# Moving solve steps, gate stores and row loads, and unscaled keys with a per-token factor on DVE in the delta rule

## The chip, the cores and the metric

The kernel runs on one core of a Trainium2 chip. The metric is the device time in microseconds of one execution, as the median of several. PE is TensorE, DVE VectorE, ACT ScalarE, POOL GpSimd, SP SyncE, which here issues all DMA.

## The reference

One layer of a streaming encoder, float32: a prompt of 4096 frames of width 1024, and 8 running streams with 16 new frames each. Two head groups of 8 heads of 64 run side by side; group A is a gated delta rule, group B softmax attention over a band of nine chunks of 64. The part that matters is group A for the prompt, in 64 chunks of 64 frames:

```python
gc = jnp.cumsum(g, axis=-1)
decay = jnp.exp(jnp.where(incl, gc[..., :, None] - gc[..., None, :], -jnp.inf))
kk = jnp.einsum('bhnid,bhnjd->bhnij', k, k)
lower = jnp.where(strict, beta[..., :, None] * kk * decay, 0.0) + jnp.eye(blen, dtype=f32)
rhs = jnp.concatenate([v * beta[..., None], k * (beta * jnp.exp(gc))[..., None]], axis=-1)
sol = lax.linalg.triangular_solve(lower, rhs, left_side=True, lower=True)
u, w = sol[..., :dv], sol[..., dv:]
qk = jnp.einsum('bhnid,bhnjd->bhnij', q, k) * decay
q_dec = q * jnp.exp(gc)[..., None]
k_tail = k * jnp.exp(gc[..., -1:] - gc)[..., None]
g_tot = jnp.exp(gc[..., -1])
def step(s, xs):                      # one chunk
    v_new = u_c - jnp.einsum('bhld,bhde->bhle', w_c, s)
    o_c = jnp.einsum('bhld,bhde->bhle', qd_c, s) + jnp.einsum('bhij,bhje->bhie', qk_c, v_new)
    s = s * gt_c[..., None, None] + jnp.einsum('bhld,bhle->bhde', kt_c, v_new)
    return s, o_c
```

q and k are L2-normed; k's norm enters as a factor per token.

## The kernel before

The kernel is a row of phases, each a block of five instruction streams that meet at semaphores, with a barrier between them. Every matmul of the projections is done as three products of float32 parts (`matmul3`, lines 88 to 90).

**Phase A** (`project_a`, to 782 us in the profile) projects q, k, v and the gates of group A, 256 tokens per block, does the convolution, and stores the activations (`qkvB`), the products k k^T and q k^T (`kq`), the sums of squares of the queries (`ssqT`), and per head and chunk the summed decays (`gcC`) and betas (`betaC`). `store_gates` writes these last two; the chunks lie in DRAM in the order of `slot(n)`: in 32 chunks first the 16 even ones, then the odd ones.

**Phase B** (`project_b`, 782 to 1730 us) projects the other columns for 33 tiles of 128 tokens in 165 units; a unit is one tile times 512 columns, 24 matmuls into one of five PSUM banks (`BANKS`). The units begin with Q of tiles 0 and 1, K of tiles 0 and 1, then Q and K of tile 2. Per tile SP loads x (`load_x`, line 1056), ACT rounds it (`split_hi`, line 1230), DVE takes the rest (`split_lo`, line 1315). PE waits for `lo_ok` ahead of a tile, and for `normed` of five units earlier ahead of a bank. Per Q or K unit ACT squares, DVE sums (line 1371), POOL takes the power (lines 1196, 1200), DVE scales (line 1376).

Between the units the other engines solve the triangular systems of the 64 chunks, in four groups of 16 chunks x 8 heads = 128 systems, one per partition (`solve_plan`, `solve(u)` of each stream). A planner lays out the steps: each engine has a list in fixed order, each step a cost, each unit a `budget(k, u)` per engine, and a step comes in the first unit in which its needs are planned. `PRE = 4` units (-4 to -1) lie ahead of unit 0. In them, before the change, SP issues `lgb` (decays and betas, line 1084), `lkk` (2 MB of k k^T into M, line 1090), `lqk` and `seg` (line 1109), DVE does `ssk` (line 1327, waits for `lkk`) and the two differences `dd` (line 1338), ACT `init` and `eg`, POOL the four powers `pow` (line 1165). In unit 0 DVE does `rows` (line 1345), which waits for the powers. The first `load_x` inside the units is that of tile 2, at the end of unit 2 in SP's order.

**The delta rule** (`delta`, 1730 to 2083 us) goes through 64 chunks, two per tile. SP loads per tile the factors (`sc`, line 1564: the keys' and the queries' factor per token, broadcast over 64 partitions), the solved matrices `UQ`, the gate rows `za` and per two tiles the raw q, k, v (`conv_T`, line 1554), six tiles ahead. Once, `ketr` and `ssqT` come into `rows` (lines 1582, 1583), are transposed by PE (line 1776) and copied by DVE (line 1840). Per tile POOL multiplies keys and queries by their factors (`scaled`, line 1619: `Kd`, `Qd`), gates and norms the output; PE transposes keys and values (`prepare`, lines 1716, 1718), ACT copies the values (`vt`, line 1659), DVE scales the transposed keys (`kt`, line 1808). The loop per chunk, each step for two halves of four heads: PE `Kd` x state into `psS` (`keys_state`, line 1735); DVE r = vt - psS (`residual`, line 1819); PE solves (`solved`, line 1754); ACT copies the new values (line 1668); PE takes their product with `kt` (`new_state`, line 1771); DVE adds the decayed state (`state`, line 1831). Queries times state (line 1746) and the outputs (line 1762) lie between them in PE's order; DVE sums the squares of a tile's output (`out_sums`, line 1837) after the state of its next even chunk.

Behind it come the delta rule of the samples, the attention and the output projections.

## Time and profile before

| | |
|---|---|
| median of 3 runs | 3701.06 us (3700.84 to 3708.35) |
| profiled execution | 3700.53 us, span 3698.8 us |
| mean granted TensorE clock | 0.961 |
| PE busy | 3406.3 us, 92% of the span |
| DVE busy | 2123.7 us, 57% |
| ACT busy | 1388.1 us, 38% |
| POOL busy | 1023.8 us, 28% |

The span runs from the first to the last instruction of the slowest core. An engine is busy while it works on data; waits are not counted. In a row of a timeline the first number is the start, the second the time to the end of the group, "x2" the number of instructions in it, and the bracket holds how long the engine had been idle and whose result came last ("issue": no releaser found). PEld is the loading of weights into TensorE. The clock is granted in parts of full speed, 1.00 being 2.4 GHz and 0.50 1.2 GHz.

### The profile page before, as it was taken

The numbers are of one execution on the slowest core, as the hardware profiler recorded it, in microseconds if no ns is written. First come the engines' busy times: TensorE is split into PE (matmuls) and PEld (weight loads), VectorE is DVE, ScalarE is ACT, GpSimd is POOL, SyncE is SP. The second block draws the span as 40 slices with busy tenths as digits, with TensorE's granted clock in tenths as the row PEclk, the third lists the DMA queues.
The fourth block names the chain that finished last, engine by engine and source line by source line (L and its number), as shares of the span: only waits on it lengthen the run. The fifth ranks groups of instructions, "written<-read, shape, count | busy, mean of one in ns | idle before, by whom it ended". The sixth has DMA issues, their size and how long they took to land. (4 is left out here: it accounts for less than half of the span.)

```text
span 3698.8 us, 68754 instructions
## 1 busy us (share of the span) xinstructions
PE 3406.3 (92%) x26606; PEld 2912.4 (79%) x26606; DVE 2123.7 (57%) x4024; ACT 1388.1 (38%) x2648; POOL 1023.8 (28%) x1313
## 2 busy tenths in 40 slices
PE   6999999959998999997888577999997999999998
PEld 6999899948887888885777455888885888888887
DVE  7777687747988968760344454666664233333332
ACT  5555555533223322211565424666663111111111
POOL 3222122238997644400687510000000000000000
PEclk9999999979999999998898788999998999999999
DMA  5343333355347453434987443222224121212120
GB/s 152 107 117 104 101 110 107 96 145 156 112 121 212 133 161 102 122 106 131 252 253 240 120 143 121 84 76 77 82 67 171 61 68 61 68 61 68 61 68 36
DMA packets 320091, 428.30 MB, mean 116 GB/s; under 512 B 189539, under 2 KB 204163, under 8 KB 315190
## 3 DMA queue, kind: packets, MB, share of 16 engines
q1 hardware_dynamic: 319806, 424.43, 38.0%
q8 instruction: 187, 3.06, 0.3%
q14 instruction: 98, 0.80, 0.1%
HBM read 267.51 MB, written 159.46 MB: 115 GB/s over the span
## 5 line engine op out<-in xcount | busy, mean ns | idle before, releaser
L88 PE MATMUL b_psP<-b_w_hi,b_xT_hi 128*128 128x512 f32 x1320 | 518.7, 393 | 45.3 <-DVE b_xT_lo L1315 28.2
L89 PE MATMUL b_psP<-b_w_lo,b_xT_hi 128*128 128x512 f32 x1320 | 516.4, 391 | 0.0
L90 PE MATMUL b_psP<-b_w_hi,b_xT_lo 128*128 128x512 f32 x1320 | 515.8, 391 | 0.0
L88 PE MATMUL a_psG<-a_xT_hi,a_w_hi 128*128 128x256 f32 (+1 forms) x1536 | 454.3, 296 | 21.0 <-DVE a_xT_lo L670 19.5
L89 PE MATMUL a_psG<-a_xT_lo,a_w_hi 128*128 128x256 f32 (+1 forms) x1536 | 442.0, 288 | 0.0
L90 PE MATMUL a_psG<-a_xT_hi,a_w_lo 128*128 128x256 f32 (+1 forms) x1536 | 441.3, 287 | 0.0
L88 PEld LDWEIGHTS b_psP<-b_w_hi,b_xT_hi 128*128 128x128 f32 x1320 | 249.3, 189 | 104.3 <-DVE b_xT_lo L1315 53.0
L88 PEld LDWEIGHTS a_psG<-a_xT_hi,a_w_hi 128*128 128x128 f32 x1536 | 296.0, 193 | 42.7 <-DVE a_xT_lo L670 23.5
L687 DVE SCALAR_TENSOR_TENSOR a_act<-a_raw,a_taps,a_act 128x256 f32<-128x256 f32 x576 | 288.9, 502 | 20.6
L90 PEld LDWEIGHTS a_psG<-a_xT_hi,a_w_lo 128*128 128x128 f32 x1536 | 296.3, 193 | 0.0
L89 PEld LDWEIGHTS a_psG<-a_xT_lo,a_w_hi 128*128 128x128 f32 x1536 | 296.2, 193 | 0.0
L90 PEld LDWEIGHTS b_psP<-b_w_hi,b_xT_lo 128*128 128x128 f32 x1320 | 249.5, 189 | 52.7
L89 PEld LDWEIGHTS b_psP<-b_w_lo,b_xT_hi 128*128 128x128 f32 x1320 | 249.5, 189 | 51.4
L3128 POOL TENSOR_SCALAR h_var<-h_ssq 128x1 f32<-128x1 f32 x33 | 6.3, 191 | 865.8 <-ACT h_squares L3160 865.8
L2637 DVE CUSTOM_DVE_ANT_0 f_neg<-f_score,f_bias 128x640 f32<-128x640 f32 (+4 forms) x256 | 192.4, 780 | 81.9 <-PE f_score L2537 52.9
L410 POOL COPY a_halo<-a_raw 128x3 f32<-128x3 f32 x192 | 74.1, 386 | 509.6 <-ACT a_raw L515 508.2
L88 PE MATMUL h_psH<-h_w_hi,h_mT_hi 128*128 128x512 f32 x528 | 210.0, 398 | 5.1 <-DVE h_w_lo L107 5.1
L2456 ACT ACTIVATE f_prob<-f_neg,f_low 128x640 f32<-128x640 f32 (+4 forms) x256 | 201.2, 788 | 17.9 <-DVE f_low L2637 17.9
L1036 DVE TENSOR_TENSOR b_tmp_v<-b_M,b_col_v 128x62 f32<-128x62 f32 (+28 forms) x464 | 205.7, 483 | 3.6
L90 PE MATMUL h_psH<-h_w_hi,h_mT_lo 128*128 128x512 f32 x528 | 207.1, 392 | 0.0
L89 PE MATMUL h_psH<-h_w_lo,h_mT_hi 128*128 128x512 f32 x528 | 207.0, 392 | 0.0
L90 PE MATMUL h_psG<-h_w_hi,h_hT_lo 128*128 128x512 f32 x528 | 205.5, 389 | 0.0
(365 smaller groups left out, 7373.8 us busy)
## 6 DMA issues: line engine op xcount, KB each, us to landing
rows_b<-b_rows SPq DMA_DIRECT2D x165, 256.0 KB, 2.2
b_x_full<-xT SPq DMA_DIRECT2D x78, 512.0 KB, 4.2
qkvB<-a_act SPq DMA_DIRECT2D x16, 1536.0 KB, 5.4
d_conv_T<-qkvB SPq DMA_DIRECT2D x16, 1536.0 KB, 11.9
xT<-a_x_full SPq DMA_DIRECT2D x33, 512.0 KB, 3.6
h_mixed<-mixed SPq DMA_DIRECT2D x33, 512.0 KB, 4.1
out<-h_y SPq DMA_DIRECT2D x33, 512.0 KB, 3.0
a_x<-in_x_prompt SPq DMA_DIRECT2D x32, 512.0 KB, 4.1
```

Source lines behind the costliest of these rows:

```text
L88: nc.tensor.matmul(out, x_hi, w_hi, start=first, stop=False)
L89: nc.tensor.matmul(out, x_hi, w_lo, start=False, stop=False)
L90: return nc.tensor.matmul(out, x_lo, w_hi, start=False, stop=last)
L410: pool.tensor_copy(halo[:, g, :], x[:, N:]).then_inc(halo_ok, 1)
L687: v.scalar_tensor_tensor(out, x[:, j:j + N], taps[:, j, g:g + 1], out, ALU.mult, ALU.add).then_inc(conv, 1)
L1036: eng.tensor_tensor(t, U[:, c0:c1, j:j + 1].to_broadcast([P, c1 - c0, L]), factor.unsqueeze(1).to_broadcast([P, c1 - c0, L]), ALU.mult).th ...
L2456: e.activation(prob[h % 4][:, 0:n], neg[h % 2][:, 0:n], ACT.Exp, scale=-1.0, bias=low[a.b][:, h:h + 1], accum_out=total[a.b][:, h:h + 1]). ...
L2637: v.tensor_tensor_reduce(neg[h % 2][:, 0:n], score[h % 2][:, 0:n], bias[:, h, KEYS - n:], -1.0 / ROOT, BIG, ALU.add, ALU.min, low[a.b][:, ...
L3128: g.tensor_scalar(var[:, :], ssq[:, :], 1.0 / D, EPS, ALU.mult, ALU.add).then_inc(e_var, 1)
```

## The change

1. **Gates.** `gcC` and `betaC` are stored in the natural order of the chunks, two stores each instead of four; `lgb` puts them in the order of the groups with four loads each instead of one.
2. **Solve steps.** In the units ahead of unit 0 only SP has a budget. The steps of DVE, POOL and ACT begin in unit 0. The loads of x for tiles 2 and 3 (`LEAD = 2`) go ahead of SP's first solve steps.
3. **Unscaled keys.** The tensor `kqrow` becomes `krow` and `qrow`. `sc` holds the queries' factor alone; POOL's `Kd` is gone, and `keys_state` multiplies the raw keys. `krow` comes into `rows` and is transposed with the others; DVE copies and negates it (`key_gain`), and the residual is computed as psS x (-factor of the token) + vt, one `scalar_tensor_tensor` of 64 columns per head. The wait for `g_kd` is gone; the load of raw tiles also waits for `t_sk`.
4. **Row loads.** The eight loads of `ketr` and `krow` and that of `ssqT` go ahead of the loads of tile 0.

```diff
@@ def store_gates(q):
-                    for e in range(2):
-                        for odd in range(2):
-                            at = slot(n * b + odd)
-                            sp.dma_start(there[at:at + n // 2, e * PAIRS:(e + 1) * PAIRS].rearrange("n h i -> h n i"),
-                                         x[e::2, :].rearrange("h (n o i) -> h n o i", o=2, i=C)[:, :, odd, :]).then_inc(ok, 16)
+                        sp.dma_start(there[n * b:n * (b + 1), e * PAIRS:(e + 1) * PAIRS].rearrange("n h i -> h n i"),
+                                     x[e::2, :].rearrange("h (n i) -> h n i", n=n)).then_inc(ok, 16)
@@ project_b, budget(k, u):
+        if u < 0:
+            return 100.0 if k == "sp" else 0.0
         if k == "v":
             return 4.0 if u < HEADS else 5.0
         if k == "g":
-            return 5.0 if u < 0 else 2.8 if u < HEADS else 4.8
+            return 2.8 if u < HEADS else 4.8
@@ project_b, sync, solve(u):
                     if kind == "lgb":
                         for x, src in ((gcl, d.gcC), (betal, d.betaC)):
-                            sp.dma_start(x[:, :, :], src.rearrange("(g n) h i -> (n h) g i", g=GROUPS)).then_inc(gb_in, 16)
+                            by_group = src.rearrange("(a n e) h i -> a e n h i", e=2, n=CC)
+                            for g in range(GROUPS):
+                                sp.dma_start(x[:, g, :], by_group[g // 2, g % 2]).then_inc(gb_in, 16)
@@ project_b, sync:
+            for n in range(LEAD):
+                load_x(n + 2)
             for u in range(-PRE, 0):
                 solve(u)
             for u, (n, seg) in enumerate(units):
-                if u == ends[n] and n + 2 < len(visits):
+                if u == ends[n] and LEAD <= n < len(visits) - 2:
                     load_x(n + 2)
@@ delta, sync:
             def load_raw(x):
                 if x >= 3:
                     sp.wait_ge(t_prep, 2 * (x - 2))
                     sp.wait_ge(g_qd, 2 * (x - 2))
+                    sp.wait_ge(t_sk, 2 * 2 * 2 * (x - 2))
...
+            for n in range(NCH // 16):
+                for first, src in ((0, d.ketr), (2 * H, d.krow)):
+                    there = rows[first:first + H, n // 2 * 32 * C:(n // 2 + 1) * 32 * C]
+                    sp.dma_start(there.rearrange("h (c e i) -> h c e i", e=2, i=C)[:, :, n % 2, :],
+                                 src[16 * n:16 * (n + 1)].rearrange("c h i -> h c i")).then_inc(rows_in, 16)
+            sp.dma_start(rows[H:2 * H, :], d.ssqT).then_inc(rows_in, 16)
             for t in range(BUFS):
                 if t % 2 == 0:
                     load_raw(t // 2)
                 load(t)
@@ delta, gpsimd, scaled(t):
-                for out_, x, first, done in ((Kd, 0, PAIRS, g_kd), (Qd, 1, 0, g_qd)):
+                g.tensor_tensor(Qd[t % 2]..., raw(t)[:, 0:PAIRS, :]..., sc[b][:, :, :, :], ALU.mult).then_inc(g_qd, 1)
@@ delta, tensor, keys_state(n, x):
                 pe.wait_ge(v_state, 2 * n + x + 1)
-                if x == 0 and n % 2 == 0:
-                    pe.wait_ge(g_kd, t + 1)
                 for p, e, h, at, rows_e in half_heads(x):
-                    last = nc.tensor.matmul(psS[x][c, e, p - 2 * x, :], Kd[t % 2][rows_e, p, c], old[rows_e, p, :],
+                    last = nc.tensor.matmul(psS[x][c, e, p - 2 * x, :], raw(t)[rows_e, PAIRS + p, c], old[rows_e, p, :],
@@ delta, vector, residual(n):
-                    v.tensor_tensor(r[c, at].rearrange("p (a e c) -> p e a c", a=2, e=2),
-                                    vt[t % 2][c, at].rearrange("p (a e c) -> p e a c", a=2, e=2), psS[x][c, :, :, :],
-                                    ALU.subtract).then_inc(v_r, 1)
+                    for a in range(2):
+                        for e in range(2):
+                            p = 2 * x + a
+                            cols = slice((2 * p + e) * C, (2 * p + e + 1) * C)
+                            h = e * PAIRS + p
+                            op = v.scalar_tensor_tensor(r[c, cols], psS[x][c, e, a, :], key_gain[c, t, h:h + 1], vt[t % 2][c, cols],
+                                                        ALU.mult, ALU.add)
+                    op.then_inc(v_r, 1)
@@ delta, vector, once:
-            v.tensor_copy(scal[:, :, :].rearrange("p t h -> p (t h)"), psA[:, 0:NT * 2 * H]).then_inc(v_scal, 1)
+            part = NT // 2
+            for i, src in enumerate((psA, psB)):
+                v.tensor_copy(scal[:, i * part:(i + 1) * part, :].rearrange("p t h -> p (t h)"), src[:, 0:part * 3 * H])\
+                    .then_inc(v_scal, 1)
+            v.tensor_scalar(key_gain[:, :, :], scal[:, :, 2 * H:], -1.0, None, ALU.mult).then_inc(v_key, 1)
```

## Rows read from the trace of the kernel before

**Rows 1.** Stretches: us; busy PE, PEld, DVE, ACT, POOL; PEclk, DMA share, GB/s.
```profile
782.00:1730.00 948.00, 909.53 (x3960) 746.84 (x3960) 696.52 (x1258) 265.36 (x342) 527.43 (x494) 0.98 0.46 137
1730.00:2083.00 353.00, 267.12 (x5408) 243.98 (x5408) 130.96 (x324) 183.67 (x512) 251.73 (x229) 0.87 0.75 218
```

**Rows 2.** Timeline around the start of phase B; start, us, engine, line, tiles.
```profile
761.11 0.35 SPq L299 DMA_DIRECT2D qkvB<-a_act  x1
...
793.47 1.31 SPq L1090 DMA_DIRECT2D b_M<-kq  x1
...
804.24 2.73 SPq L1056 DMA_DIRECT2D b_x_full<-xT  x2
...
807.80 0.22 DVE L1327 TENSOR_SCALAR b_kvar<-b_M 128x64 f32<-128x64 f32 x1 [8.28 <-DMA b_M<-kq]
...
808.19 13.53 POOL L1165 TENSOR_TENSOR b_rk<-b_kvar,b_neg_half 128x16 f32<-128x16 f32 x4 [26.36 <-DVE b_decays L1332]
...
821.75 0.23 DVE L1345 TENSOR_TENSOR b_krow<-b_decays,b_rk 128x64 f32<-128x64 f32 x1 [8.58 <-POOL b_rk L1165]
...
826.40 1.53 DVE L1315 TENSOR_TENSOR b_xT_lo<-b_x_full,b_xT_hi 128x1024 fp32r<-128x1024 f32 x1
...
827.99 0.80 PE L88 MATMUL b_psP<-b_w_hi,b_xT_hi 128*128 128x512 f32 x1 [15.30 <-DVE b_xT_lo L1315]
```

**Rows 3.** One stretch of 10 us, columns as in rows 1.
```profile
795.00:805.00 10.00, 10.00 (x46) 8.29 (x45) 4.52 (x8) 4.92 (x8) 0.00 (x0) 1.00 0.89 334
```

**Rows 4.** Timeline of the start of the delta rule.
```profile
1731.43 0.42 SPq L1554 DMA_DIRECT2D d_conv_T<-qkvB  x1
...
1734.99 2.72 SPq L1582 DMA_DIRECT2D d_rows<-ketr  x4
...
1737.75 2.72 SPq L1583 DMA_DIRECT2D d_rows<-ssqT  x1
...
1746.45 1.26 POOL L1619 TENSOR_TENSOR d_Kd<-d_conv_T,d_sc 128x512 f32<-128x512 f32 x1 [9.49 <-DMA d_UQ<-UQ]
...
1751.65 3.56 PE L1776 MATMUL d_psA<-d_ident,d_rows 16*128 16x16 f32 x32 [25.11 <-DMA d_rows<-ssqT]
...
1756.07 1.12 PE L1716 MATMUL d_psA<-d_ident,d_conv_T 128*128 128x128 f32 x4 [0.86 <-DVE d_scal L1840]
```

**Rows 5.** Timeline of DVE, one undisturbed tile of the delta rule.
```profile
1850.81 0.69 DVE L1837 TENSOR_REDUCE d_oss<-d_osq 128x8 f32<-128x512 f32 x1 [0.83 <-ACT d_osq L1681]
...
1859.26 0.69 DVE L1837 TENSOR_REDUCE d_oss<-d_osq 128x8 f32<-128x512 f32 x1 [0.83 <-ACT d_osq L1681]
```

**Rows 6.** Timeline of one chunk: the residual, and its second half on PE.
```profile
1863.78 0.74 DVE L1819 TENSOR_TENSOR d_r<-d_vt,d_psC 64x256 f32<-64x256 f32 x2 [0.70 <-ACT d_vt L1659]
...
1864.94 0.43 PEld L1754 LDWEIGHTS d_psC<-d_r,d_UQ 64*64 64x64 f32 x6
```

**Rows 7.** Groups by line and a timeline row: xcount, busy us, mean ns of one.
```profile
L1819 DVE TENSOR_TENSOR d_r<-d_vt,d_psC 64x256 f32<-64x256 f32 x128 | 49.0, 416 | 34.5 <-ACT d_vt L1659 20.8 <-PE d_psC L1735 12.8
...
L2968 DVE SCALAR_TENSOR_TENSOR g_both<-g_psO,g_own_inv,g_part 128x64 f32<-128x64 f32 x8 | 2.3, 284 | 0.3
...
2099.05 3.23 DVE L2201 SCALAR_TENSOR_TENSOR e_conv_T<-e_work,e_taps,e_conv_T 128x128 f32<-128x128 f32 x12
```

**Rows 8.** A disturbance on PE, and the sums of squares on DVE.
```profile
1808.16 0.69 PE L1771 MATMUL d_psC<-d_vn,d_kt 64*64 64x64 f32 x8 [3.21 <-issue]
...
1956.54 0.69 DVE L1837 TENSOR_REDUCE d_oss<-d_osq 128x8 f32<-128x512 f32 x1 [0.91 <-ACT d_osq L1681]
...
L1837 DVE TENSOR_REDUCE d_oss<-d_osq x32: 677/686/689, 1772.1 to 2075.4; 128x8 f32<-128x512 f32 x32
```

**Rows 9.** Stretches of 100 us of the delta rule, columns as in rows 1.
```profile
1757.00:1857.00 100.00, 80.73 (x1552) 73.67 (x1551) 37.18 (x92) 52.60 (x148) 66.74 (x60) 0.85 0.93 253
...
1857.00:1957.00 100.00, 82.84 (x1724) 75.14 (x1719) 41.72 (x103) 59.28 (x166) 80.84 (x73) 0.93 0.78 242
...
1957.00:2057.00 100.00, 84.42 (x1807) 77.23 (x1807) 43.44 (x108) 60.87 (x171) 83.29 (x75) 0.93 0.65 199
```

More of the change, by code:

```diff
@@ L252, in stores_of @@
         def stores_of(upto):
-            return sum(32 if b is None else 128 for b in sets[:upto])
+            return sum(32 if b is None else 64 for b in sets[:upto])
         def weights_ready(eng, upto):
@@ L1104, in solve @@
                         sp.wait_ge(v_rows, 3 * (n + 1))
-                        for x, there in ((krow, d.kqrow[:, :, 0]), (ketr, d.ketr)):
+                        for x, there in ((krow, d.krow), (ketr, d.ketr)):
                             sp.dma_start(there[chunks].rearrange("n h i -> (n h) i"), x[:, :]).then_inc(sc_out, 16)
@@ L1235, in solve @@
                     if kind == "init":
-                        e.wait_ge(gb_in, 32)
+                        e.wait_ge(gb_in, 32 * GROUPS)
                         e.activation(egl, gcl[:, :, :], ACT.Exp).then_inc(s_init, 1)
@@ L1328, in solve @@
                                         ALU.mult, ALU.add).then_inc(v_ssk, 1)
-                        v.wait_ge(gb_in, 32)
+                        v.wait_ge(gb_in, 32 * GROUPS)
                         if n:
@@ L1334, in solve @@
                     elif kind == "dd":
-                        v.wait_ge(gb_in, 32)
+                        v.wait_ge(gb_in, 32 * GROUPS)
                         if n:
@@ L1461, in delta @@
         UQ = some("UQ", [P, H, 2, C])
-        sc = some("sc", [P, 2, PAIRS, 2, C])
-        rows = ph.sb("d_rows", [2 * H, s.SEQ])
+        sc = some("sc", [P, 2, PAIRS, C])
+        rows = ph.sb("d_rows", [3 * H, s.SEQ])
         za = some("za", [P, W], ZBUFS)
-        Kd = some("Kd", [P, PAIRS, P], 2)
         Qd = some("Qd", [P, PAIRS, P], 2)
@@ L1468, in delta @@
         vt = some("vt", [P, W], 2)
-        scal = ph.sb("d_scal", [P, NT, 2 * H])
+        scal = ph.sb("d_scal", [P, NT, 3 * H])
+        key_gain = ph.sb("d_key_gain", [P, NT, H])
         S = some("S", [P, PAIRS, C], 2)
@@ L1501, in delta @@
         v_scal = ph.sem("d_v_scal")
+        v_key = ph.sem("d_v_key")
         v_kt = ph.sem("d_v_kt")
         s_vt = ph.sem("d_s_vt")
-        g_kd = ph.sem("d_g_kd")
         g_qd = ph.sem("d_g_qd")
@@ L1563, in load @@
                     half = slice(e * C, (e + 1) * C)
-                    sp.dma_start(sc[b][half, :, :, :, :],
-                                 kqrow[t // 16, :, t % 16, e * PAIRS:(e + 1) * PAIRS].partition_broadcast(C)).then_inc(ok, 16)
+                    sp.dma_start(sc[b][half, :, :, :],
+                                 qrow[t // 16, :, t % 16, e * PAIRS:(e + 1) * PAIRS].partition_broadcast(C)).then_inc(ok, 16)
                 sp.dma_start(UQ[b][:, :, :, :], d.UQ[:, :, t].rearrange("e j h x i -> (e j) h x i")).then_inc(ok, 16)
@@ L1578, in _ @@
                 load(t)
-                if t == 0:
-                    for n in range(NCH // 16):
-                        there = rows[0:H, n // 2 * 32 * C:(n // 2 + 1) * 32 * C].rearrange("h (c e i) -> h c e i", e=2, i=C)
-                        sp.dma_start(there[:, :, n % 2, :], d.ketr[16 * n:16 * (n + 1)].rearrange("c h i -> h c i")).then_inc(rows_in, 16)
-                    sp.dma_start(rows[H:2 * H, :], d.ssqT).then_inc(rows_in, 16)
             for t in range(NT):
@@ L1617, in scaled @@
                     g.wait_ge(t_qs, 2 * 2 * (t - 1))
-                for out_, x, first, done in ((Kd, 0, PAIRS, g_kd), (Qd, 1, 0, g_qd)):
-                    g.tensor_tensor(out_[t % 2][:, :, :].rearrange("p a (c i) -> p c a i", c=2),
-                                    raw(t)[:, first:first + PAIRS, :].rearrange("p a (c i) -> p c a i", c=2),
-                                    sc[b][:, :, :, x, :], ALU.mult).then_inc(done, 1)
+                g.tensor_tensor(Qd[t % 2][:, :, :].rearrange("p a (c i) -> p c a i", c=2),
+                                raw(t)[:, 0:PAIRS, :].rearrange("p a (c i) -> p c a i", c=2),
+                                sc[b][:, :, :, :], ALU.mult).then_inc(g_qd, 1)
             def gate(t):
@@ L1772, in new_state @@
                 last.then_inc(t_ds, 1)
-            pe.wait_ge(rows_in, 16 * (1 + NCH // 16))
+            pe.wait_ge(rows_in, 16 * (1 + NCH // 8))
             for t in range(NT):
-                last = nc.tensor.transpose(psA[:, t * 2 * H:(t + 1) * 2 * H], rows[:, t * P:(t + 1) * P], ident[0:2 * H, 0:2 * H])
+                to = (psA, psB)[t // (NT // 2)]
+                at = t % (NT // 2) * 3 * H
+                last = nc.tensor.transpose(to[:, at:at + 3 * H], rows[:, t * P:(t + 1) * P], ident[0:3 * H, 0:3 * H])
             last.then_inc(t_rows, 1)
-            pe.wait_ge(v_scal, 1)
+            pe.wait_ge(v_scal, 2)
             prepare(0)
@@ L3327, in build @@
     d.gcC, d.betaC, d.ketr = (scratch(k, [NCH, s.HA, s.DV]) for k in ("gcC", "betaC", "ketr"))
-    d.kqrow = scratch("kqrow", [NCH, s.HA, 2, s.DV])
+    d.krow, d.qrow = (scratch(k, [NCH, s.HA, s.DV]) for k in ("krow", "qrow"))
     d.gt = scratch("gt", [NCH, s.HA])
```

9 lines of the change are left out of this document (5 added, 4 removed).

## The prediction

> **What bounds the kernel now.** I read the views in this order: the engine table of the page, the stretches by phase, the timelines of the two phase borders that the change touches, then one tile of the delta rule on DVE and PE, and last the long idle times of PE. The table shows PE as the busiest engine by far, so what counts is where PE is idle: 948 - 910 = 38 us in phase B (782 to 1730) and 353 - 267 = 86 us in the delta rule (1730 to 2083) [rows 1]. Of the 38 us in phase B, 15.30 are one gap, from 812.69 to 827.99, ahead of the product with the third input tile [rows 2]. In the delta rule PE is not the limit but one link of a loop of PE, DVE, PE, ACT, PE, DVE that runs 64 times: a tile of two chunks takes 1859.26 - 1850.81 = 8.45 us where nothing disturbs it [rows 5]. From the first to the last of its 32 sums of squares (1772.1 to 2075.4) it took 303.3 us for 31 tiles [rows 8], against 31 x 8.45 = 262: 41 us are disturbances.
>
> **Gate stores of phase A.** Eight small stores per block of 256 tokens become four with the same bytes in the same runs of 256 bytes. In the last block SP was through with them before 761.11, when it issued the store of qkvB after a wait for ACT [rows 2]; the 2.5 us that it now saves lie under that wait. I take 0, at most 1.5 us of gain in a middle block. The loads of decays and betas become 8 instead of 2.
>
> **Start of phase B.** Before, DVE, POOL and ACT ran preparation steps of group 0 ahead of the first unit. DVE then sat idle 8.58 us for POOL's four powers (13.53 us from 808.19 on), and only behind that came the sums, the scaling and the split at 826.40 for which PE waited [rows 2]. The loads of input tiles 2 and 3 went at 804.24, behind SP's own waits [rows 2]. Now they go at some 792 and 795, the three engines start their steps inside the units, and the powers lie one per unit. Late next is `ssk`, now in unit 0: it waits for the 2 MB load of M, which had landed at 807.80 [rows 2]. M is now issued at 795.2 + 8 x 0.44 = 798.7 instead of 793.47, but before it queued behind the weights. At the 334 GB/s of that time [rows 3] 2 MB need 6.3 us: it lands at 807 to 811, and I take 808.5. From there on DVE needs 4.7 us for `ssk` and the two differences (from 807.80 to 821.75 - 8.58 - 0.67 = 812.5), 3.2 for the sums, POOL's variance and power of the heads and the scaling (the 4.65 from 821.75 to 826.40 hold one such pair more, and bound it), and 1.5 for the split: PE starts again at 817.9 and has waited 5 us, not 15.3. I take 10 us of gain, from 6 (M at 812) to 13 (PE's clock, which fell in the long gap, stays up). Behind that POOL has more work per unit (3.4 for a power and some 3 for the heads) than PE (some 5.3: 24 products at 46 in 10 us [rows 3]), for four units; the five PSUM banks cover these 4 us. All later solve steps move 4 units back at the start and 2 at the end (the planner's last step is in unit 155 of 165, not 153), still ahead of PE's last unit. How they then meet the single-product units is open: 0, within 4 us either way.
>
> **Start of the delta rule.** PE waited 25.11 us for the rows of factors, whose loads are issued from 1734.99 to 1740.47, behind those of tile 0, and turned them from 1751.65 on. Tile 0 itself had landed at 1746.45, when POOL begins on it, but PE's first transpose of keys came at 1756.07 [rows 4]. Now 8 loads of 0.68 us and `ssqT` are issued from 1731.4 to 1737.5 (1739.5 if `ssqT` is held up 2.72 us as before [rows 4]), then tile 0. Its loads took 1746.45 - 1731.43 = 15 us with 2.8 MB; with half the bytes of query factors they need 13, from 1738.5 on: 1751.5. The transposes of the rows, the copies (two instead of one) and the negation lie under that. I take 4.5 us of gain, from 0 (the short runs hold the queue) to 8.
>
> **The residual, on the path.** Per chunk, two subtractions of 64x256 become eight operations of 64x64 with a factor per partition, four behind each of the two semaphore counts. The pair takes 0.74 us and one of them 0.416 [rows 6, 7]: the second starts 0.33 behind the first. The sums of squares take 0.686 for 512 columns [rows 8], so 256 columns cost 0.27, 64 cost 0.067, and 0.06 to 0.07 of the 0.33 are fixed. The nearest row to the new form is g_both: the same operation, a PSUM input, a factor by pointer, 64 columns, 0.284 us for one. How closely such operations follow each other shows in e_conv_T: 12 of 128 columns in 3.23 us [rows 7], at 0.284 + 0.067 = 0.35 for one, so (3.23 - 0.35) / 11 = 0.262; less 0.067 for half the columns that is 0.195. So the first half is ready after 3 x 0.195 + 0.284 = 0.87 us instead of 0.42, the second after 7 x 0.195 + 0.284 = 1.65 instead of 0.74. Not all of these 0.91 us are on the path. PE takes the second half 1.16 us behind the start of the residual (1864.94 against 1863.78 [rows 6]), 0.42 after it is ready, because it is still at the first half and the queries. It will now be ready at 1.65 and taken at 1.72: 0.56 later. All that follows (new values, new state, output rows, the copy of the next values) hangs on that product, and the scaling of the keys on DVE still ends ahead of the state's addition. 64 x 0.56 = 36 us. The ends are 64 x 0.27 = 17, if the operations follow at 0.067 + 0.07 us, and 64 x 0.91 = 58, if PE has no slack.
>
> **Keys without POOL.** POOL loses a product per tile, of its 252 us in 353 [rows 1]. In the waits of PE's key products POOL does not appear as a releaser, so I take 0; if it does limit some tile, 0 to 3 us of gain.
>
> **What comes back.** The 41 us of disturbances are times in which PE is idle with no releaser in the profile; 3.21 us at 1808.16 is the longest of nine above 1 us [rows 8]. They are frequent where DMA is full: the 8 tiles up to 1859.26 lost 19.6 us at a DMA share of 0.93, the 10 up to 1956.54 12.8 us at 0.78, the last 13 9.0 us at 0.65 [rows 5, 8, 9]. My reading, which no row shows, is that PE's instructions are loaded through the same engines. Then a slower loop gives each such load 0.7 us more lead, and the load on DMA falls to 2.05 / 2.30 MB per tile over 9.57 / 8.45 us, 0.79. With an assumed mean delay of 2.5 us beyond the lead, exp(-0.3) x 0.79 = 0.58 of the 41 us remain, 24, and 17 come back. The ends are 0 and 25. Against it speaks SP's new wait on t_sk: a raw tile's load (1.5 MB) now goes only after the keys of a tile's second chunk, in one burst with the loads queued behind it on SP. It is needed five tiles later, so nobody waits for it.
>
> The Trainium skill, VectorE: DVE Perf Modes, section on the TRN2 errata, says that a vector operation pays a fixed extra per instruction and advises 512 elements and more. That speaks against this change, and the trace agrees: some 0.07 us per subtraction, 0.13 with a pointer.
>
> **The sum** against the profiled run of 3700.5 us (span 3698.8): 0 - 10 - 4.5 + 36 - 17 = +4.5, or 3705. The median of the runs shown is 0.5 us above that run, so 3705 stands for it too.
>
> **Rivals.** (1) Slower: the disturbances do not depend on pace or bytes, nothing comes back, and the time is 3705 + 17 = 3722. For it: they fall into bursts of loads that remain, and the raw load joins them. Against it: their fall with the DMA share. From 3.5 us less given back than forecast the change is slower. (2) The new operations do not overlap on DVE, each holds it for its 0.284 us; the second half is ready after 2.27 and taken at 2.31, 1.15 later per chunk: 74 us, 3743. The e_conv_T row speaks against it. The Trainium skill has it as a rule (VectorE: DVE Perf Modes, "The DRAIN you can't avoid": the next operation waits until the pipe is empty); by that rule it would be 3743, and the trace does not agree. (3) Faster: the operations follow at 0.14 us, or PE has more slack than the one chunk shows; the path grows by 17 us, and 3700.5 - 14.5 + 17 - 18 = 3685. For it: the price of the pointer rests on one pattern. (4) Phase B does not start as the change says: M lands after 817, `ssk` blocks DVE, and the gap stays; 3715.
>
> **How the numbers follow.** Forecast 0.40, rival 1 0.18, rival 2 0.05, rival 3 0.30, rival 4 0.07. A measurement of this kernel can tell 0.2% (7.4 us) from no change, so the bounds are 3693.7 and 3708.5. The forecast has 3694 to 3716 of its own: 0.27 of it counts as same, 0.13 as slower. Rival 3 gives 0.26 faster and 0.04 same, rival 4 0.01 same. Faster 0.26, same 0.32, slower 0.13 + 0.18 + 0.05 + 0.06 = 0.42. The range takes in rivals 1, 3 and 4 with half their width and leaves out rival 2: 3682 to 3729.
>
> **What would show it.** The residual's operations 0.2 us apart, and an undisturbed tile of 9.5 to 9.6 us. PE idle near 5 us ahead of unit 4. The first transpose of keys 4 to 5 us earlier after the delta rule's start. Shorter idle times of PE without a releaser; if they still sum up to 40 us, the step on what comes back is wrong. If a clean tile is under 9.2 us, the step on spacing or slack is wrong. If PE's clock in undisturbed tiles falls below 1.00, all of it is off.

## The result and the profile after

The kernel after takes 3681.3 us (median of 6 runs, 3675.4 to 3685.8) against 3701.2 us for the kernel before beside it (3699.6 to 3710.2): ratio 0.9942, 95% interval 0.9927 to 0.9957. The forecast was 3705 us and, as its likeliest sign by a little, slower. The change is faster by 20 us, and 3681.3 lies just below the lower end of the range, 3682. The profiled execution of after took 3679.84 us, its span is 3678.1.

I divide the two spans at the same four borders: the first matmul of phase B, the first instruction of the delta rule on DVE (the clearing of the state), the first product of keys and state, and the last addition to the state.

| part | before, us | after, us | difference | forecast |
|---|---|---|---|---|
| phase A, to the first matmul of phase B | 788.5 | 780.3 | -8.2 | 0 |
| phase B | 942.2 | 936.5 | -5.7 | -10 |
| start of the delta rule | 27.3 | 19.0 | -8.3 | -4.5 |
| its loop, 64 chunks | 314.4 | 316.0 | +1.6 | +19 (36 - 17) |
| the rest | 1626.4 | 1626.3 | 0 | 0 |

Two stretches of after (phase B, delta rule), columns as in rows 1, to be held against rows 1:

```profile
780.00:1716.00 936.00, 910.49 (x3960) 747.89 (x3960) 693.90 (x1257) 264.81 (x341) 522.14 (x494) 0.99 0.44 137
1716.00:2062.00 346.00, 259.45 (x5408) 234.68 (x5408) 189.63 (x710) 183.12 (x512) 212.32 (x197) 0.93 0.64 199
```

DVE does 59 us more in the delta rule and POOL 39 less, as the diff says. What rows 1 did not lead me to expect is the seventh number, behind the five busy times: PE's granted clock rose from 0.87 to 0.93 there.

**Phase A.** SP and ACT around the second block, first before, then after (timelines):

```profile
77.32 2.75 SPq L316 DMA_DIRECT2D gcC<-a_gc  x4
80.11 2.49 SPq L316 DMA_DIRECT2D betaC<-a_beta  x4
83.13 11.09 SPq L288 DMA_DIRECT2D kq<-a_kq  x8
...
89.60 0.60 ACT L471 ACTIVATE a_kq<-a_psK 128x512 f32<-128x512 f32 x1 [6.56 <-DMA kq<-a_kq]
```

```profile
76.86 1.50 SPq L314 DMA_DIRECT2D gcC<-a_gc  x2
78.40 1.22 SPq L314 DMA_DIRECT2D betaC<-a_beta  x2
80.16 10.23 SPq L288 DMA_DIRECT2D kq<-a_kq  x8
...
86.64 0.60 ACT L469 ACTIVATE a_kq<-a_psK 128x512 f32<-128x512 f32 x1 [4.07 <-DMA kq<-a_kq]
```

Behind the gate stores SP's queue holds the stores of k k^T (line 288). ACT can't copy the next product out of PSUM until its buffer is stored, and PE waits for ACT. The stores now go 3 us earlier, and ACT's wait shrinks from 6.56 to 4.07 us. PE's waits for that copy in all of phase A, before and then after (us in total, times, longest):

```profile
PE a_psK L602 <- ACT a_kq L471: 13.2, 5, 5.1
PE a_psK L600 <- ACT a_kq L469: 9.4, 4, 3.2
```

They are 3.8 us shorter. PE's busy time fell by another 3.8 us for the same matmuls (723.6 to 719.8, mean clock 0.97 and 0.98), so here too the clock adds to the wait. The gain comes in few of the 16 blocks: SP issues the first gate stores 0.5 us earlier (77.32, 76.86), the second 5.9 (118.99, 113.07), and all from the eleventh on 8.1 (539.00, 530.92).

**Start of phase B** in after (timeline), to be held against rows 2:

```profile
780.33 0.77 PE L88 MATMUL b_psP<-b_w_hi,b_xT_hi 128*128 128x512 f32 x1 [16.67 <-DVE b_w_lo L1314]
...
794.21 0.57 SPq L1092 DMA_DIRECT2D b_M<-kq  x1
...
801.92 0.22 DVE L1331 TENSOR_SCALAR b_kvar<-b_M 128x64 f32<-128x64 f32 x1 [9.24 <-DMA b_M<-kq]
...
809.92 1.22 DVE L1319 TENSOR_TENSOR b_xT_lo<-b_x_full,b_xT_hi 128x1024 fp32r<-128x1024 f32 x1
...
811.19 0.80 PE L88 MATMUL b_psP<-b_w_hi,b_xT_hi 128*128 128x512 f32 x1 [6.28 <-DVE b_xT_lo L1319]
```

**Start of the delta rule** in after (timeline), to be held against rows 4:

```profile
1717.85 0.39 SPq L1583 DMA_DIRECT2D d_rows<-ketr  x1
...
1721.21 0.35 SPq L1559 DMA_DIRECT2D d_conv_T<-qkvB  x1
...
1726.21 1.87 PE L1781 MATMUL d_psA<-d_ident,d_rows 24*128 24x24 f32 x16 [13.54 <-DMA d_rows<-ssqT]
...
1733.93 1.09 PE L1721 MATMUL d_psA<-d_ident,d_conv_T 128*128 128x128 f32 x4 [4.15 <-DMA d_UQ<-UQ]
```

**The loop** in after: the residual of a chunk and the two ends of a clean tile (timeline of DVE), to be held against rows 5 and 6:

```profile
1857.82 1.62 DVE L1829 SCALAR_TENSOR_TENSOR d_r<-d_psC,d_key_gain,d_vt 64x64 f32<-64x64 f32 x8 [0.70 <-ACT d_vt L1664]
...
1999.92 0.69 DVE L1847 TENSOR_REDUCE d_oss<-d_osq 128x8 f32<-128x512 f32 x1 [0.83 <-ACT d_osq L1686]
2009.46 0.69 DVE L1847 TENSOR_REDUCE d_oss<-d_osq 128x8 f32<-128x512 f32 x1 [0.83 <-ACT d_osq L1686]
```

A clean tile takes 2009.46 - 1999.92 = 9.54 us, where the forecast had 9.57. The disturbances are what changed beyond the forecast. The waits of PE in the loop, before (1758 to 2072) and then after (1736 to 2052): what for, us in total, times, longest.

```profile
PE d_psC L1754 <- DVE d_r L1819: 22.8, 48, 1.3
PE d_psC L1771 <- issue: 12.9, 5, 3.2
PE d_psO L1762 <- issue: 6.1, 2, 3.3
PE d_psO L1746 <- issue: 4.0, 4, 1.7
```

```profile
PE d_psC L1757 <- DVE d_r L1829: 54.0, 64, 1.8
PE d_psO L1749 <- issue: 1.8, 2, 1.6
PE d_psA L1721 <- issue: 1.6, 2, 1.2
```

The wait for the residual grew by 31 us. The idle times without a releaser ("issue") fell from 28 us in all to 4.

And a clean tile of before beside a disturbed one (stretches, columns as in rows 1):

```profile
1934.56:1943.00 8.44, 6.51 (x161) 5.84 (x157) 4.04 (x11) 5.71 (x17) 7.82 (x8) 1.00 0.84 287
1943.00:1956.54 13.54, 10.60 (x173) 9.74 (x174) 4.12 (x11) 5.72 (x17) 8.20 (x8) 0.77 0.62 175
```

The disturbed tile is 5.1 us longer. It holds two idle times without a releaser, 1.65 and 1.67 us. PE's granted clock was 0.77, a mix of its levels of 2.4 and 1.2 GHz, and the same work kept it busy for 10.60 us instead of 6.51, which is 4.1 of the 5.1 us; its idle time as a whole grew by only 1.0, since it waited less for DVE. So a disturbance is a stall plus a stretch at the lower clock.

The traces also show what PE waits for in a stall. The profile has DMA queues of the kind "instruction", queue 8 among them. Its line on the profile's page of before and of e_more, a run below with 1024 more matmuls and so 2048 more instructions for PE (packets, MB, share):

```profile
q8 instruction: 187, 3.06, 0.3%
q8 instruction: 195, 3.19, 0.4%
```

That is one packet of 16 KB more for every 256 more instructions of PE: queue 8 brings PE's instructions, through the same 16 DMA engines as the loads. In the loop of before it moves 43 packets. One of them stands in the stretch from 1805 to 1806 us (packets, MB, share), and the stall of 3.21 us in rows 8 ends at 1808.16:

```profile
q8 instruction: 1, 0.02, 6.8%
```

All 16 stalls of 0.3 us or more in this loop end 2.2 to 3.0 us behind a packet of queue 8, and so do all 5 of after, all 13 of e_plain_bytes, all 9 of e_more and the one of e_noload. With 43 packets in 314 us, one moment in nine would lie so by chance. The stalls are PE's own instructions coming late. The stretch right behind the stall of rows 8 (columns as in rows 1) shows the clock that follows:

```profile
1808.16:1814.00 5.84, 5.84 (x68) 5.39 (x69) 2.42 (x5) 0.97 (x3) 5.68 (x7) 0.52 1.03 307
```

### The profile page after: what moved, and what is told of

Read it like the earlier page. It is cut to its first block and busy times, and to the rows that moved or that the text cites. A ratio compares the mean times of both kernels' runs of the same rounds, so it can differ in the third digit from the quotient of the medians.

```text
span 3678.1 us, 69025 instructions
## 1 busy us (share of the span) xinstructions
PE 3394.7 (92%) x26606; PEld 2899.7 (79%) x26606; DVE 2181.8 (59%) x4410; ACT 1388.4 (38%) x2650; POOL 979.1 (27%) x1281
## 5 line engine op out<-in xcount | busy, mean ns | idle before, releaser
L1282 ACT ACTIVATE b_rows<-b_psP 128x512 f32<-128x512 f32 x99 | 59.3, 599 | 390.6 <-PE b_psP L90 382.8
```

The costliest lines, as they stand in the source:

```text
L1282: e.activation(rows[u % ROWS][:, :], psP[u % BANKS][:, :], ACT.Copy if seg == V else ACT.Silu).then_inc(taken, 1)
```

## Experiments

In all runs L is the loop, from the first product of keys and state to the last addition to the state. T is a clean tile, the spacing of two sums of squares where nothing disturbs. D = L - 32 T are the disturbances. In this measure D is 44 us before (314.4 - 32 x 8.445) and 11 after (316.0 - 32 x 9.54). The expectations speak of these. "issue" is what the waits of PE show without a releaser within L. The medians' ratios are to the kernel before on the same chip.

| kernel | T | L | D | of it issue | PE's mean clock in L | ratio of medians (95%) |
|---|---|---|---|---|---|---|
| before | 8.445 | 314.4 | 44 | 28 | 0.91 | 1 |
| e_gates | 8.445 | 314.6 | 44 | 29 | 0.91 | 0.9987 (0.9975 to 0.9999) |
| e_steps | 8.445 | 315.7 | 45 | 27 | 0.89 | 0.9996 (0.9983 to 1.0008) |
| e_all_kd | 8.445 | 320.3 | 50 | 33 | 0.90 | 0.9963 (0.9949 to 0.9978) |
| e_twice | 9.12 | 322.9 | 31 | 15 | 0.91 | 1.0028 (1.0011 to 1.0044) |
| e_slowres | 9.545 | 319.2 | 14 | 7 | 0.96 | 1.0020 (1.0010 to 1.0029) |
| e_plain_bytes | 8.445 | 316.0 | 46 | 24 | 0.88 | 0.9962 (0.9947 to 0.9977) |
| e_mixed | 8.63 | 315.3 | 39 | 26 | 0.92 | 0.9969 (0.9955 to 0.9984) |
| e_plain | 8.445 | 292.9 | 23 | 13 | 0.94 | 0.9911 (0.9887 to 0.9935) |
| e_four | 9.445 | 319.3 | 17 | 3 | 0.92 | 0.9974 (0.9956 to 0.9991) |
| after | 9.54 | 316.0 | 11 | 4 | 0.96 | 0.9942 (0.9927 to 0.9957) |
| e_more | 9.545 | 327.3 | 22 | 10 | 0.93 | 0.9990 (0.9976 to 1.0003) |
| e_noload | 8.445 | 279.9 | 10 | 4 | 0.96 | 0.9899 (0.9876 to 0.9922) |
| e_dummy | 9.97 | 350.7 | 32 | 5 | 0.87 | 1.0121 (1.0096 to 1.0146) |

D comes from one profiled execution each. How far it varies shows in the five kernels with the fast residual and all factors loaded: 44, 44, 45, 46, 50. The profiled execution is not always a typical one: that of e_all_kd is 8 us above the median of its kernel, those of e_dummy, e_more, e_plain and e_mixed are 10, 6, 5 and 3 below. D of these five can be off by as much.

The runs also show how far the other parts vary. Phase A up to the first matmul of phase B takes 786.1 to 789.2 us in the six kernels with the old gate stores (mean 787.6) and 780.2 to 783.5 in the eight with the new ones (mean 781.0). Phase B takes 942.2 to 946.3 us in the six kernels with the old solve steps (mean 944.8) and 936.4 to 942.1 in the eight with the new ones (mean 939.3).

### The gate stores alone

```diff
-                        for odd in range(2):
-                            sp.dma_start(there[at:at + n // 2, ...
+                        sp.dma_start(there[n * b:n * (b + 1), ...
...
+                            for g in range(GROUPS):
+                                sp.dma_start(x[:, g, :], by_group[g // 2, g % 2]).then_inc(gb_in, 16)
```

> The kernel before with only the gate stores in natural order and the eight loads of decays and betas. If the gate stores hold up the stores of k k^T behind them on SP: phase B's first product at 780 to 781 instead of 788.5, the gap ahead of its third input tile 0 to 3 us longer, total 3692 to 3695 against 3700.5. If the 8 us have another origin: first product at 788 to 789, total 3700 to 3703.

Phase B starts at 781.05 instead of 788.49, and ACT's wait in the second block is the 4 us of after (timeline of this run):

```profile
87.12 0.60 ACT L469 ACTIVATE a_kq<-a_psK 128x512 f32<-128x512 f32 x1 [4.04 <-DMA kq<-a_kq]
```

The whole gains 4.8 us by the medians and 4.1 by the spans, a little less than expected (3696.1 against 3692 to 3695); phase B and the parts behind it were some 3 us longer in this execution. So the gate stores alone bring phase A's gain, which settles the first theory.

### The solve steps alone

```diff
+        if u < 0:
+            return 100.0 if k == "sp" else 0.0
...
+            for n in range(LEAD):
+                load_x(n + 2)
```

> The kernel before with only the moved solve steps and the early loads of input tiles 2 and 3. If the moved steps alone explain phase B: PE's gap ahead of the third input tile 5 to 7 us instead of 15.3, phase B 5 to 7 us shorter, phase A and the delta rule's loop as before, total 3694 to 3696. If the eight smaller loads of decays matter for it: gap over 8 us, total 3698 or more.

PE's first gap in phase B is 6.76 us, as expected, but phase B lasts 942.1 us, as before, and not 5 to 7 us less. A part of its gain is given back some 290 us later, where PE waits again for the low part of x from DVE. PE's waits there (timeline of this run) are two of a row of seven between 1104 and 1171 that sum to 14.7 us:

```profile
1104.53 0.50 PE L88 MATMUL b_psP<-b_w_hi,b_xT_hi 128*128 128x512 f32 x1 [2.67 <-DVE b_xT_lo L1319]
...
1125.53 0.50 PE L88 MATMUL b_psP<-b_w_hi,b_xT_hi 128*128 128x512 f32 x1 [2.75 <-DVE b_xT_lo L1319]
```

The kernel before has four in that stretch (5.55, 0.84, 0.96 and 1.86), 9.2 us. PE's waits of 0.6 us and more in all of phase B sum to 27.0 us before, 25.6 here and 21.0 in after. By these waits, of the 8.5 us won at the start 1.4 stay here, and of 9.0 in after 6. That step of the prediction expected 10 to stay. But this pair of executions is at the edge of both groups: before has the shortest phase B of the six kernels without the moved steps, e_steps the longest of the eight with them. By the means above the steps bring 5.5 us. Why the later waits grow (11.7 us before, 18.8 here, 14.7 in after) was not tested by a run.

### The slow residual alone

```diff
-                    v.tensor_tensor(r[c, at]..., vt[t % 2][c, at]..., psS[x][c, :, :, :], ALU.subtract).then_inc(v_r, 1)
+                    for a in range(2):
+                        for e in range(2):
+                            op = v.scalar_tensor_tensor(r[c, cols], psS[x][c, e, a, :], key_gain[c, t, h:h + 1], vt[t % 2][c, cols],
+                                                        ALU.mult, ALU.add)
+                    op.then_inc(v_r, 1)
```

`key_gain` is set to -1 here.

> The kernel before with the residual computed as in the kernel after (eight operations of 64 columns, factor -1), with keys scaled by POOL, all bytes and all orders as before. A clean tile must be 9.54 us, 305 for 32. If a slower loop by itself takes the disturbances away (pace): they fall from 44 us to 11 to 15 and the total is 3700 to 3706. If bytes, POOL or the raw loads' wait do it: they stay at 40 to 44 us and the total is 3731 to 3735. By the split of the prediction (0.74 by pace, 0.79 by bytes): 33 us, 3724.

All loads, POOL's keys and the order are those of before; only the pace is that of after. D falls from 44 to 14 us and the kernel loses 6 to 7 us, where the slower tiles alone would cost 35. Both the time (3707.1) and D are as expected from pace, up to 1 us. A stretch of 100 us shows it (columns as in rows 1), to be held against the DMA-heavy stretches of rows 9:

```profile
1898.00:1998.00 100.00, 79.23 (x1730) 71.57 (x1729) 61.40 (x231) 59.30 (x167) 80.28 (x73) 1.00 0.77 243
```

DMA is as busy as before (0.77 against 0.78 in the middle stretch of rows 9), yet the clock stays at 1.00. Of this D most lies in the first four tiles (14.67, 12.71, 10.60 and 11.14 us), while the six tiles in advance are still being loaded.

### Everything but the unscaled keys

The kernel before with the gate stores, the solve steps, the row loads ahead of tile 0 and SP's wait for `t_sk`.

```diff
+                    sp.wait_ge(t_sk, 2 * 2 * 2 * (x - 2))
...
-                if t == 0:
-                    for n in range(NCH // 16):
+            for n in range(NCH // 16):
```

> The kernel before with the gate stores, the solve steps, the row loads ahead of tile 0 and the raw loads' wait for t_sk of the kernel after, but with its own residual and POOL's scaled keys. If pace takes the disturbances away in the kernel after: 40 us or more of them stay here, loop 312 to 318, total 3678 to 3684. If the raw loads' wait does it: disturbances near 12, loop 282, total 3646 to 3652. If bytes or POOL do it: as for pace; these are told apart by other runs.

D is 50 us, so the later raw loads do not help. The loop (320.3) and the total (median 3690.3) are above the 312 to 318 and 3678 to 3684 expected. From the clearing of the state to the first transposes of keys it takes 20.4 us. The seven kernels with the old order of row loads take 23.4 to 25.4, the other six with the new order, e_plain_bytes (18.3) with all bytes of the factors among them, 17.2 to 18.6. So the order of the row loads brings most of the gain there. The bytes of tile 0 are at most a small part; what the 2 us between this run and the other six are was not tested.

### A fast residual with the traffic of after

```diff
-                    for a in range(2):
-                        for e in range(2):
-                            op = v.scalar_tensor_tensor(...)
+                    v.tensor_tensor(r[c, at]..., vt[t % 2][c, at]..., psS[x][c, :, :, :], ALU.subtract).then_inc(v_r, 1)
```

> The kernel after with its residual replaced by the two plain subtractions of before; the key's factor is left out there, and the factors copied by DVE are made 1000 times smaller so that the numbers stay finite. Fast pace (clean tile 8.45 us), half the bytes of factors, no scaled keys on POOL. If pace alone decides: disturbances back at 40 to 46 us, loop 310 to 316, total 3674 to 3682. If fewer bytes and less POOL work take them away too: disturbances under 25, loop under 296, total under 3663.

D is 23 us: half of the disturbances stay away at the fast pace, and the loop takes 292.9 us, so a loop of 315 is no floor. The time is 0.9911 of before (median 3667.7, above the 3663 expected), but it is no solution, since the key's factor is missing.

### The same with both factors loaded

```diff
-        sc = some("sc", [P, 2, PAIRS, C])
+        sc = some("sc", [P, 2, PAIRS, 2, C])
...
-                                 qrow[t // 16, :, t % 16, e * PAIRS:(e + 1) * PAIRS]...
+                                 kqrow[t // 16, :, t % 16, e * PAIRS:(e + 1) * PAIRS]...
```

> The run e_plain (kernel after, two plain subtractions, key's factor left out) with both factors loaded per tile again as in the kernel before; POOL still makes no scaled keys. Clean tile 8.45 us. If the bytes of the factors make the difference between 23 us of disturbances (e_plain) and 44 to 50 (before, e_all_kd): 38 to 50 us here, loop 308 to 320. If POOL's scaled keys make it: 20 to 28 us, loop 290 to 298.

D is back at 46 us and the ratio of medians 0.5% higher, which is 19 us and so a little less than the 23 us of D. POOL still makes no scaled keys, so these cost nothing that the medians show: 0.9962 without them, 0.9963 with them in e_all_kd. The stretch (columns as in rows 1) of this run and that of e_noload, below, are 100 us each:

```profile
1860.00:1960.00 100.00, 87.59 (x1699) 79.85 (x1699) 41.35 (x103) 58.57 (x166) 69.77 (x64) 0.85 0.83 257
```

### Without the loads

```diff
-                if t % 2 == 1 and t // 2 + 3 < NT // 2:
-                    load_raw(t // 2 + 3)
-                if t + BUFS < NT:
-                    load(t + BUFS)
```

The first six tiles are used again and again.

> The kernel before with the delta rule's loads from tile 6 on left out: the six tiles already in SBUF are used again and again. Clean tile 8.45 us. If traffic of the kernel's own loads delays PE's instructions: the disturbances of 44 us shrink to those of the first tiles, 5 to 15 us, loop 275 to 285. If PE's instructions come at a rate of their own (a tile in some 9.4 us, whatever the loads do): disturbances 35 to 44, loop 305 to 314.

```profile
1860.00:1960.00 100.00, 87.84 (x1995) 80.12 (x1991) 47.42 (x119) 68.23 (x191) 92.73 (x85) 1.00 0.10 34
```

At the fast pace all tiles but the first two or three are clean, and the 10 us of D lie there, while the six tiles are loaded. The disturbances of the kernel before are made by the loads. The 43 packets of PE's instructions come here too, so a pace that PE's instructions can't exceed for themselves is ruled out.

### More instructions for PE

```diff
+                if x == 0:
+                    for i in range(8):
+                        e, p = i % 2, i // 2 % PAIRS
+                        nc.tensor.matmul(psO_all[c, e, PAIRS * C + 16 * p:PAIRS * C + 16 * (p + 1)], Qd[t % 2][rows_e, p, c],
+                                         old[rows_e, p, 0:16], start=False, stop=False)
```

> The kernel after with eight more small matmuls (16 columns, into unused PSUM columns) per chunk, in the time in which PE waits for DVE: 32 more instructions for PE per tile of about 340, clean tile 9.5 to 9.9 us. If PE's supply of instructions has a ceiling (340 in some 9.4 us), a tile now needs 10.3 us of it: disturbances come back, 15 to 30 us beyond after's 11, loop 330 to 345. If only the pace of the loop counts: disturbances stay near 11, loop 316 to 325.

A clean tile stays 9.55 us, and neither loads nor pace changed, but D doubles from 11 to 22 us, in an execution 6 us below its kernel's median. The expected 15 to 30 beyond 11 were missed from below, the rival's "near 11" from above, and so was the loop: 327.3, between 316 to 325 and 330 to 345. It goes the way of the reading that the stalls are PE's own instructions coming late behind the loads. One execution against the spread of 44 to 50 above is no proof of the size; the packets of queue 8, 51 instead of 43 in this loop, with one 2.3 to 2.8 us ahead of the end of each of its nine stalls, carry the reading.

### Slowing the loop in two other ways

e_twice does each subtraction twice, e_dummy one addition of idle data ahead of the residual.

```diff
+                    v.tensor_tensor(spare[c, at]..., vt[t % 2][c, at]..., psS[x][c, :, :, :], ALU.subtract).then_inc(v_spare, 1)
```

> The kernel before with each of its two subtractions done twice (first into an unused tile): the same form of operation, 0.66 us more DVE time per chunk, the second half ready 3 x 0.33 + 0.42 = 1.4 us behind the start instead of 0.74; a clean tile of 8.9 to 9.2 us, all loads and POOL's work as before. If pace counts whatever slows it: disturbances 20 to 32 us, loop 312 to 320, total 3699 to 3706. If the form of the residual counts: 40 us or more, loop 326 to 336, total over 3711.

```diff
+                    if x == 0:
+                        v.tensor_tensor(idle[1][c, :], idle[0][c, :], idle[0][c, :], ALU.add).then_inc(v_idle, 1)
```

> The kernel before with one more DVE operation per chunk (an addition of 480 columns of idle data, some 0.55 us) ahead of the residual, which stays two subtractions. A clean tile must come to 9.5 to 9.6 us. If it is the pace of the loop that takes PE's idle times without releaser away, whatever slows it: disturbances 10 to 16 us as with the slow residual (13), loop 317 to 321, total 3703 to 3708. If it is the form of the residual (how DVE reads PSUM): disturbances stay at 40 us or more, total 3731 to 3736.

e_twice keeps the form of the residual and D falls to 31 us at 9.12 us per tile, between 44 at 8.45 and 14 at 9.55; its loop (322.9) and its time (3709.4) are a few us over the ranges given. So it is the pace and not the form. e_dummy is slower than either theory had it, 3745 us. Its added operation took 0.66 us in a tile's first chunk and mostly 0.92 to 1.18 in the second, which makes T 9.97. Its stalls are gone as expected (5 us of 28 are left, all before 1811), but D is 32 us, not the 10 to 16 expected from pace: some 23 of them lie in the tiles from 1821.82 on, which have no stall at all. They lost clock without stalls (stretches, columns as in rows 1; a disturbed tile, and a clean one):

```profile
2060.14:2071.65 11.51, 9.40 (x169) 8.70 (x168) 5.53 (x13) 5.72 (x17) 8.74 (x7) 0.79 0.07 24
2094.54:2104.50 9.96, 7.57 (x186) 6.76 (x184) 5.53 (x12) 5.71 (x17) 6.26 (x5) 1.00 0.08 28
```

DMA is nearly idle in both tiles, and PE waits only for DVE (0.75 and 1.26 us in the first). Still the clock fell, in groups of one to six tiles up to the end, and did so alike under loads and without. So a slower pace takes the stalls away, but not always the disturbances: the clock is a second cause that needs neither a load nor a stall. Why it fell here and hardly in e_slowres, where PE waits 54.6 us for the residual against 69.4 here, is open.

### Two attempts at a faster kernel

e_mixed scales the keys of the first half of the heads on POOL and leaves the second half to the factor on DVE. e_four multiplies in PSUM by the broadcast factors, two operations of 64x256, and then subtracts.

```diff
+                    if x == 0:
+                        v.tensor_tensor(r[c, at]..., vt[t % 2][c, at]..., psS[x][c, :, :, :], ALU.subtract).then_inc(v_r, 1)
+                        continue
```

> The kernel after, but the first half of the heads has its keys scaled by POOL and one plain subtraction again, and only the second half has the four operations with a factor. The second half is then ready 0.33 + 0.585 + 0.284 = 1.2 us behind the residual's start, where PE took it at 1.16 before: a clean tile of 8.5 to 8.7 us. Loads and POOL's work lie halfway between before and after. If disturbances hang on pace and traffic together: 28 to 38 us of them, loop 303 to 313, total 3670 to 3680, below both kernels. If they take back all that pace gives (after's loop is a floor): loop 314 to 320, total 3680 to 3686.

```diff
+                    v.tensor_tensor(psS[x][c, :, :, :], psS[x][c, :, :, :],
+                                    gain_of(t, x)[c].unsqueeze(3).to_broadcast([C, 2, 2, C]), ALU.mult).then_inc(v_m, 1)
```

> The kernel after with the key's factor applied in another form: two multiplications of 64x256 in PSUM by the broadcast factors, then two subtractions of 64x256. First half ready 2 x 0.33 + 0.42 = 1.08 us behind the start instead of 0.87, second half 3 x 0.33 + 0.42 = 1.41 instead of 1.65; a clean tile of 9.0 to 9.2 us instead of 9.54. Loads and POOL's work as after. If disturbances follow pace and traffic: 12 to 20 us of them (after 11, the run e_plain at 8.45 us per tile 23), loop 302 to 312, total 3668 to 3678. If the loop has a floor near 315: 315 to 318 and a total of 3680 to 3684.

Neither beats after: their times are 3690.9 and 3686.9 us, above the ranges of both theories. In e_mixed T is 8.63 as worked out, but D is 39, a little over the range given: L is 315.3, that of before and after, as the floor of the loop would have it. The 292.9 us of e_plain speak against such a floor. e_four came to 9.445 us per tile instead of 9.0 to 9.2, and its loop of 319.3 is above both ranges (timeline of a chunk, with the keys' product on PE first; then the lengths of the single operations, shortest, median, longest in ns):

```profile
1855.46 1.00 PE L1739 MATMUL d_psC<-d_S,d_conv_T 64*64 64x64 f32 x16
1855.98 0.94 DVE L1823 TENSOR_TENSOR d_psC<-d_psC,d_scal 64x256 f32<-64x256 f32 x2
1856.84 0.73 DVE L1832 TENSOR_TENSOR d_r<-d_vt,d_psC 64x256 f32<-64x256 f32 x2
...
L1823 DVE TENSOR_TENSOR d_psC<-d_psC,d_scal x128: 415/430/444, 1741.0 to 2055.7; 64x256 f32<-64x256 f32 x128
L1832 DVE TENSOR_TENSOR d_r<-d_vt,d_psC x128: 402/413/426, 1741.7 to 2056.5; 64x256 f32<-64x256 f32 x128
```

The pair of multiplications takes 0.94 us here where the pair of subtractions takes 0.73, so the second half is ready after 1.59 us, not 1.41. One operation that reads and writes PSUM is hardly longer than a subtraction (0.43 against 0.41 us). The pair is longer in this chunk since its second operation starts at 1856.49, right when the second half of the keys' product ends (1856.46); in the other chunk of a tile the pair takes 0.78 or 0.79 us in clean tiles.

## Why the prediction was wrong

**What comes back** is the step that failed most. The prediction's reading was that PE's instructions come late behind the loads, so that loads and pace together set the disturbances. It holds: the stalls end behind packets of PE's instructions, and loads (e_noload, e_plain against e_plain_bytes) and pace (e_slowres, e_twice) both move them. The size of the term was off. By the sums of squares the 41 us became 5.7 (2053.97 - 1752.53 = 301.4 us less 31 x 9.54), not 24; a part of that is the last of these spacings, which is short in itself (6.33 us in after, 7.50 before). In the measure of the table 33 us came back, not 17. Two parts of that term fell. The share for the load on DMA was taken as proportional, 0.79, of which the bytes alone are 2.05 / 2.30 = 0.89, where the fewer bytes alone halved D (46 to 23; by the medians 19 us less). The share for pace was taken as exp(-0.3) = 0.74, from an assumed mean delay of 2.5 us, where the pace alone left 14 of 44 us, a third. And the term took a disturbance for a stall. Only 28 of the 44 us are stalls; the other 16 go with the lower clock that follows them (PE is busy 260.3 us in the loop of before and 244.7 in that of e_noload). The stalls themselves were misread a little: between 1758 and 2072 eleven are above 1 us, not nine, and the longest is 3.34 us, at 1838.67. With both parts at their measured sizes, the two effects also overlap: 10 to 14 us are left in e_slowres, in after and in e_noload alike, in e_slowres and e_noload mostly at the start.

**The gate stores** were the second miss: 0 taken, at most 1.5, and 8.2 us measured (6.6 by the means of all runs). The step looked at the last block of phase A, where indeed nothing was gained (8.1 us are won when it begins), and not at what is queued behind the stores in the other blocks. In the second block SP's next job is the one on which ACT, and through it PE, waits. These two steps make most of the miss: against the forecast, 8 us of the 25 are the gate stores and 16 what comes back.

**Start of phase B.** The gap fell to 6.28 us from 15.30, where 5 was forecast; M landed by 801.92, and PE started 9.3 us behind it, by the steps of the prediction 9.4. So rival 4 did not happen. What was off is the step on how the solve steps then meet the units, taken as 0: PE's later waits for the low part of x took a third of the gain back in after and more in e_steps. It was within the 4 us given.

**Start of the delta rule.** 8.3 us from the clearing of the state on, just beyond the 0 to 8 given. The short row loads went out in 3.4 us (1717.85 to 1721.21), not in 6: they were costed at the 0.68 us each that rows 4 show, where they queued behind tile 0's loads.

**The residual** was right: 36 us forecast; 32 x (9.54 - 8.445) = 35, and PE's wait for it 31 us longer. The trace of after has eight operations in 1.62 us with 0.28 us for one, (1.62 - 0.28) / 7 = 0.19 us apart, so they do overlap, and rival 2 did not happen. The Trainium skill's rule in the prediction (VectorE: DVE Perf Modes, "The DRAIN you can't avoid") goes on, in the same section, "A next op that is not held starts earlier", and the trace agrees with that sentence. The lower end of this step, 17 us, does not follow from its own rows: with operations 0.137 us apart the second half is ready after 1.24 us and taken after 1.31, 0.15 later than before, which is 10 us.

**Keys without POOL** cost nothing, as forecast. Rival 3, the faster case, had nearly the right time (3685) by a mechanism that did not happen: its operations were not closer than forecast. Rival 1 is refuted, since D did depend on pace and bytes. The sum with the measured sizes is -8.2 - 5.7 - 8.3 + 35 - 33 = -20 us; these are the parts of the same two executions, so it holds by the way they are cut.

## What to carry to other kernels

Where PE issues many small matmuls under heavy loads, look at the waits without a releaser together with the clock beside them: a loop can have a slower path and the same time, because the slack takes up the stalls. Shortening such a path buys little until the traffic beside it shrinks (e_plain against e_plain_bytes: 19 to 23 us for 0.25 MB of some 2.3 per tile), and lengthening it can cost little (e_slowres: 6 us for tiles that are 35 us longer in all), but need not (e_dummy: 36 us more in the loop for 49). Cost a removed DMA issue by what is queued behind it in every block, not by the wait that hides it in one.

## What the runs showed of the hardware

PE's instructions come in packets of 16 KB, one per 256 of them, through the 16 DMA engines that also carry the kernel's loads; in tiles with a DMA share of 0.6 and more they came late, and 44 of 44 stalls in five traces end 2.2 to 3.0 us behind such a packet. The same 0.25 MB less per tile took D from 46 to 23 us; the response is far from proportional. A tile with some 3 us of stalls comes with a clock of 0.77 and is 5 us longer. The clock also fell with no stall and no load (e_dummy, 0.79 at a DMA share of 0.07).

The addition of 480 columns from SBUF to SBUF on DVE took between 0.65 and 1.35 us in e_dummy, and the trace shows what stretches it: in each second chunk from 1780 on it begins while POOL is in one of its operations of 512 columns, and it takes 0.5 us more than what that operation still has to run (0.41 and 0.92 us, 0.57 and 1.08, 0.79 and 1.30). Beside POOL's operations of 8 columns it took 0.66. An operation of 64x256 on DVE that reads and writes PSUM took 0.43 us, one with the result in SBUF 0.41.
